# Two of eight chunks of three input projection units by seven block products, in a two-layer encoder trunk

## The chip, the cores and the metric

The kernel runs on one core of a Trainium2 chip. The metric is the device time of one execution in microseconds (us), launch to end. The core has TensorE (PE, matmuls), VectorE (DVE), ScalarE (ACT), GpSimd (POOL) and SyncE (SP, which here only issues DMAs), each with its own instruction stream; they are ordered by semaphores.

## What is computed

A trunk of two layers on 256 frames of width 2048, in float32. From the reference:

```python
for l in range(DEPTH):                       # DEPTH = 2
    h = rmsnorm(x, norm_mix[l])
    proj = h @ w_in[l]                       # 2048 -> 5456 columns
    qa, ka, va, qi, ki, wi, qb, kb, vb = jnp.split(proj, offsets, axis=-1)
    o_a = dsa_branch(...)                    # 8 heads x 128; an indexer of 16 heads x 64 keeps the 64 best keys
    o_b = swa_branch(...)                    # 16 heads x 64, window of 128, sinks
    gates = jax.nn.sigmoid(h @ w_gate[l])
    merged = g_a * (o_a @ w_branch_a[l]) + g_b * (o_b @ w_branch_b[l])
    x = x + merged @ w_out[l]
    h = rmsnorm(x, norm_mlp[l])
    x = x + jnp.square(jax.nn.relu(h @ w_up[l])) @ w_down[l]
return rmsnorm(x, final_norm)
```

The index score of a query and a key is `sum over heads of w * relu(qi . ki)`; the branch A softmax runs over the 64 keys with the best scores.

## The kernel before

**Arithmetic.** Every large product is taken in split form. A weight block arrives as `raw` in float32; ACT rounds it to `w_hi`, DVE subtracts to get `w_lo`, and TensorE adds three products of float32r: high by high, high activation by low weight, low activation by high weight. The activations are kept as such pairs too (`h_hl` for the normed input, `o_hl`, `m_hl`).

**Chunks.** All weights are cut into chunks of 256 rows by 512 columns, 1,024 columns in SBUF. A layer has 472 chunks, and every engine walks them in the same order: 8 narrow ones (`misc`: index keys, index weights, branch B keys and values), 80 of the input projection (from `C_WIN` = 8; ten units of eight), 96 of gates and branches (from `C_MIXA` = 88 and `C_MIXB` = 136), 32 of the output projection, 256 of the MLP. A unit is eight chunks that add up to 256 x 512 outputs in two PSUM banks. The units 0 and 1 of the input projection make the index queries, 2 and 3 branch A's queries, 4 and 5 its keys, 6 and 7 its values, 8 and 9 branch B's queries.

**A plain chunk** is twelve matmuls of 512 columns (L578 to L580: two row blocks of the weights, two halves of the frames, three products each). **A wide chunk** takes the 2 x 2 block product by seven block products for eight (`seven_products`, from L534): 21 matmuls of 256 columns (L546 to L548), out of sums of weight blocks (DVE, `weight_sums`, L1359 to L1365, written behind the raw block) and sums of activation blocks. It fills, beside the two banks of the unit, two side banks, which are joined with them once a unit: ACT copies half a bank, DVE makes five additions (`add_up_sides`, L1767 to L1775). Its high part is two ACT instructions (L929, L931) around the weight sums, its low part one DVE instruction of 1,792 columns (L1371); a plain chunk has one of 1,024 on each (L922, L1350). Before the change only gates of branch B and the MLP have wide chunks.

**Slots and order.** Four raw slots and four high/low slots rotate. ACT may write slot c once TensorE is through with chunk c - 4 (`multiplied`); SP issues the load of chunk c once DVE is through with chunk c - 4 (`lo_ready`); TensorE starts a chunk when its low part is there. So ACT and DVE run up to about three chunks ahead of TensorE: this is the lead that the text speaks of. Everything else is set by hand at a chunk of each engine's stream: `unit(...)` on ACT and DVE takes a `take` step (ahead of chunk 3's split), `then` steps (behind the split of the chunk given) and a `taken` step (behind chunk 6's).

**A finished unit** goes: ACT scales it out of PSUM into `stage` (`take_win`, L1128; units 6 and 7 into `va`), DVE transposes it in 32 x 32 pieces into `spread` (L1428), SP stores that in DRAM (L342) and fetches it in four parts into `moved` (L348), ACT copies it into place (`place`, L984). `stage`, `spread` and `moved` exist once. In a unit that is all done for the unit before: ACT and DVE at chunk 3, the store ahead of the load of chunk 7, the fetches behind it, ACT's `place` behind chunk 6.

**Jobs** lie between the chunks (`jobs_after`). On TensorE the index scores come in three visits of two rounds at `IDX_AT` = chunk 32, 36 and 40 of the layer (L673); ACT and DVE have their parts (relu, then a weighted sum over heads, L1507) `AHEAD` = 4 chunks further down their own streams. The top-k selection on DVE (`choose`, L1522 and L1524) stands behind chunks 52 to 60, the branch A jobs behind every other chunk from 64 on TensorE. The index scores use all four side banks (`att` 0 to 2, `turn`), branch A's jobs `att` 0 to 2, the narrow chunks `att` 0 and 1.

## Time and profile before

| | |
|---|---|
| time, median of 3 runs | 2658.05 us (2656.88 to 2658.99) |
| time of the profiled execution | 2658.03 us |
| its span, first to last instruction | 2656.1 us |
| TensorE busy | 2641.4 us (99%) |
| VectorE busy | 2078.8 us (78%) |
| ScalarE busy | 1448.1 us (55%) |
| DMA | 594.52 MB, mean 224 GB/s |
| granted TensorE clock, mean | 0.999 |

The busy time of TensorE can't be read as work at its peak: matmuls overlap in the records and their ends are modelled. What counts is the distance between the starts of two matmuls, and whether a start was held up by a semaphore. A row of the timeline says so in brackets: idle time before it and who released it. A row of several instructions (x2, x4) gives their common span.

### The profile page before, as it was taken

What the parts mean: (1) busy time and instruction counts of PE and PEld (TensorE: products, weight loads), DVE (VectorE), ACT (ScalarE), POOL (GpSimd) and SP (SyncE); (2) the same over time, 40 slices, a digit from 0 to 9 for tenths busy, and PEclk for the clock granted to TensorE, in tenths of its full rate; (3) what the DMA queues carried; (4) which work ended last, traced back from release to release, by engine and by line L of the source; (5) the groups of instructions that cost most, each with busy time, mean ns of one, the idle gap of its engine ahead of it and who ended that gap; (6) DMA issues with size and microseconds to landing.
All of it is one profiled execution on the core that took longest, in us unless ns stands there. A gap on an engine that the chain in (4) does not pass through costs nothing.

```text
span 2656.1 us, 37301 instructions
## 1 busy us (share of the span) xinstructions
PE 2641.4 (99%) x13432; PEld 2217.1 (83%) x13432; DVE 2078.8 (78%) x3099; ACT 1448.1 (55%) x1863; POOL 215.8 (8%) x378
## 2 busy tenths in 40 slices
PE   9999999999999999999999999999999999999998
PEld 7788778888888888888888887788888888888887
DVE  5667678967898897987756766789678989989875
ACT  5445555545565655655455455555456556556554
POOL 0103110000100100100010021100000001000000
PEclk9999999999999999999999999999999999999999
DMA  7877676666775766767777666667677767667574
GB/s 260 239 236 224 222 226 195 229 231 231 244 228 191 246 216 206 240 205 232 235 237 225 224 225 221 218 202 233 227 256 231 221 208 242 209 217 234 189 248 151
DMA packets 187395, 594.52 MB, mean 224 GB/s; under 512 B 25576, under 2 KB 46612, under 8 KB 187088
## 3 DMA queue, kind: packets, MB, share of 16 engines
q1 hardware_dynamic: 166256, 536.94, 62.1%
q0 software_dynamic: 20432, 54.86, 7.5%
q8 instruction: 106, 1.74, 0.3%
q14 instruction: 73, 0.60, 0.1%
q10 hardware_dynamic: 528, 0.37, 0.1%
HBM read 544.58 MB, written 47.48 MB: 223 GB/s over the span
## 4 chain that ended last, share of the span: by engine, by line
PE 95%; DVE 3%; DMA 1%; issue 1%; ACT 0%; DVEq 0%; POOLq 0%; POOL 0%; SPq 0%; ACTq 0%
PE acc L578 24%; PE acc L579 24%; PE acc L580 24%; PE att L546 2%; PE att L548 2%; PE att L547 2%; PE acc L546 2%; PE acc L548 2%; PE acc L547 2%; PE acc L595 1%; PE acc L594 1%; PE acc L596 1%; DMA raw<-in_w_main 1%; DVE w_lo L1350 1%; DVE w_lo L1371 1%
## 5 line engine op out<-in xcount | busy, mean ns | idle before, releaser
L1350 DVE TENSOR_TENSOR w_lo<-raw,w_hi 128x1024 fp32r<-128x1024 f32 (+1 forms) x778 | 933.2, 1211 | 374.0 <-ACT w_hi L922 370.3
L922 ACT ACTIVATE w_hi<-raw 128x1024 fp32r<-128x1024 f32 (+1 forms) x778 | 813.1, 1051 | 633.5 <-PE acc L580 462.4
L578 PE MATMUL acc<-w_hi,h_hl 128*128 128x512 f32 x1848 | 735.2, 398 | 1.1 <-DVE w_lo L1350 1.1
L580 PE MATMUL acc<-w_hi,h_hl 128*128 128x512 f32 x1848 | 728.9, 394 | 0.0
L579 PE MATMUL acc<-w_lo,h_hl 128*128 128x512 f32 x1848 | 728.6, 394 | 0.0
L578 PEld LDWEIGHTS acc<-w_hi,h_hl 128*128 128x128 f32 x1848 | 347.9, 188 | 83.0 <-issue 4.9
L580 PEld LDWEIGHTS acc<-w_hi,h_hl 128*128 128x128 f32 x1848 | 347.9, 188 | 81.3
L579 PEld LDWEIGHTS acc<-w_lo,h_hl 128*128 128x128 f32 x1848 | 348.2, 188 | 76.3
L1371 DVE TENSOR_TENSOR w_lo<-raw,w_hi 128x1792 fp32r<-128x1792 f32 x166 | 335.5, 2021 | 33.5 <-ACT w_hi L931 32.4
L578 PE MATMUL acc<-w_hi,o_hl 128*128 128x512 f32 x912 | 360.4, 395 | 0.0
L579 PE MATMUL acc<-w_lo,o_hl 128*128 128x512 f32 x912 | 360.0, 395 | 0.0
L580 PE MATMUL acc<-w_hi,o_hl 128*128 128x512 f32 x912 | 359.6, 394 | 0.0
L929 ACT ACTIVATE w_hi<-raw 128x768 fp32r<-128x768 f32 x166 | 140.3, 845 | 195.0 <-PE acc L548 110.1
L931 ACT ACTIVATE w_hi<-raw 128x1024 fp32r<-128x1024 f32 x166 | 174.9, 1054 | 86.9 <-DVE raw L1365 86.7
L580 PEld LDWEIGHTS acc<-w_hi,o_hl 128*128 128x128 f32 x912 | 171.8, 188 | 40.2
L578 PEld LDWEIGHTS acc<-w_hi,o_hl 128*128 128x128 f32 x912 | 171.6, 188 | 37.7 <-issue 1.4
L579 PEld LDWEIGHTS acc<-w_lo,o_hl 128*128 128x128 f32 x912 | 171.7, 188 | 36.3
L1359 DVE TENSOR_TENSOR raw<-raw 128x512 f32<-128x512 f32 x166 | 113.3, 683 | 21.2 <-issue 11.3
L455 POOL DMA_DIRECT2D scratch<-spread x30 | 16.9, 563 | 973.2 <-DVE spread L1428 973.2
L1428 DVE STREAM_TRANSPOSE spread<-stage 128x512 f32<-128x512 f32 x112 | 73.0, 689 | 21.8 <-ACT stage L1128 17.5
L1020 ACT ACTIVATE probs<-probs,low 128x128 f32<-128x128 f32 x96 | 41.0, 428 | 85.0 <-DVE sink_d L1592 43.8
L1363 DVE TENSOR_TENSOR raw<-raw 128x256 f32<-128x256 f32 x166 | 70.6, 425 | 5.8
(298 smaller groups left out, 3614.9 us busy)
## 6 DMA issues: line engine op xcount, KB each, us to landing
raw<-in_w_main SPq DMA_DIRECT2D x928, 512.0 KB, 4.3
scratch<-spread SPq DMA_DIRECT2D x37, 512.0 KB, 2.8
moved<-scratch SPq DMA_DIRECT2D x148, 128.0 KB, 3.2
scratch<-spread POOLq DMA_DIRECT2D x30, 512.0 KB, 3.5
moved<-scratch POOLq DMA_DIRECT2D x120, 128.0 KB, 5.0
scratch_p<-spread POOLq DMA_DIRECT2D x16, 384.0 KB, 4.6
moved<-scratch_p POOLq DMA_DIRECT2D x64, 96.0 KB, 4.3
raw<-in_w_misc SPq DMA_DIRECT2D x16, 336.0 KB, 4.0
```

The costliest lines, as they stand in the source:

```text
L546: nc.tensor.matmul(o, a_hi, hi[:, w], start=start, stop=False, skip_group_check=True)
L547: nc.tensor.matmul(o, a_hi, lo[:, w], start=False, stop=False, skip_group_check=True)
L548: return nc.tensor.matmul(o, a_lo, hi[:, w], start=False, stop=stop, skip_group_check=True)
L578: nc.tensor.matmul(o, a_hi, hi[:, kk], start=(k == 0), stop=False)
L579: nc.tensor.matmul(o, a_hi, lo[:, kk], start=False, stop=False)
L580: last = nc.tensor.matmul(o, a_lo, hi[:, kk], start=False, stop=fin)
L922: nc.scalar.activation(w_hi[s][:, 0:2 * width], raw[r][:, 0:2 * width], ACT.Copy).then_inc(hi_ready, 1)
L929: nc.scalar.activation(w_hi[s][:, 0:3 * HALF], raw[s][:, HALF:CW], ACT.Copy)
L931: nc.scalar.activation(w_hi[s][:, 3 * HALF:7 * HALF], raw[s][:, CW:2 * CW], ACT.Copy).then_inc(hi_ready, 1)
L1350: nc.vector.tensor_tensor(w_lo[s][:, 0:2 * width], raw[r][:, 0:2 * width], w_hi[s][:, 0:2 * width].bitcast(F32), ALU.subtract).then_inc(lo ...
L1359: nc.vector.tensor_tensor(r[:, 4 * HALF:6 * HALF].rearrange("p (k n) -> p k n", k=2), r[:, HALF:3 * HALF].rearrange("p (k n) -> p k n", k= ...
L1371: nc.vector.tensor_tensor(w_lo[s][:, 0:7 * HALF], raw[s][:, HALF:8 * HALF], w_hi[s][:, 0:7 * HALF].bitcast(F32), ALU.subtract).then_inc(lo ...
```

## The change

Chunks 1 and 5 of the units 1, 2 and 6 of the input projection become wide chunks, in both layers. What comes with it:

- `gate_sums(0)` and `gate_sums(2)`, which the gate stage makes later for itself, are also made in unit 0 (DVE behind the chunks 4 and 6, low parts behind chunk 6 and behind chunk 0 of unit 1; ACT's high parts behind the chunks 5 and 7), into a view of `o_hl`, `s_win`.
- The side banks are `att` 0 and 1 for unit 1, `att` 2 and `turn` for the units 2 and 6.
- Such a unit is taken in the unit after: ACT copies half a side bank ahead of chunk 3 (`win_side`), DVE joins behind chunk 3 (`add_win_sides`), ACT scales in place behind chunk 4 (`win_scale`), DVE transposes behind chunk 5. For the units 1 and 2 SP's store stands one unit further on, behind the load of chunk 2, the fetches behind that of chunk 3, ACT's `place` behind chunk 2.
- The index scores start at chunk 36 for 32, with ACT's and DVE's parts. They now also wait for the join of unit 2.
- The index keys, branch B's keys and two small tiles of the selection lie in `o_hl`, no longer in the upper half of raw slot 1, which the weight sums now use.
- Some waits of TensorE are added where a side bank or a sum is first used.

The diff, cut to its core:

```diff
-IDX_AT, IDX_STEP, IDX_ROUNDS = C_WIN + 24, 2, 6
+IDX_AT, IDX_STEP, IDX_ROUNDS = C_WIN + 28, 2, 6
...
+WIN_UNITS = (1, 2, 6)
+WIN_CHUNKS = (1, 5)
+A_GATES = 0
+W_SUMS = len(WIN_CHUNKS)
+EARLY_SIDES = len(WIN_UNITS) + A_GATES
+EARLY_WIDE = EARLY_SIDES * len(WIN_CHUNKS)
...
+        with nc.sbuf_tensor("o_room0", [P, 14 * SEQ], F32), nc.sbuf_tensor("kiT_kbT", [P, 2, SEQ], F32) as kiT_kbT, \
+                nc.sbuf_tensor("o_room1", [P, 8 * SEQ], F32), nc.sbuf_tensor("win_side_sum", [P, HALF], F32) as win_sum_room, \
+                nc.sbuf_tensor("o_room2", [P, 5 * SEQ], F32), nc.sbuf_tensor("ki2", [P, TT, 2, I_DIM], F32) as ki2, \
+                nc.sbuf_tensor("best8", [P, TOPK // 8, 8], F32) as best8:
+            pass
+        win_side_sum = win_sum_room[:, :]
...
+        s_win = o_hl[:, :, 10:14, :].rearrange("p a k s -> p a (k s)").rearrange("p a (b c) -> p a b c", b=W_SUMS)
...
+        win_sides = dict(zip(WIN_UNITS, (wide_acc[0], wide_acc[1], wide_acc[1])))
...
+                    then = {}
+                    if u - 2 in WIN_UNITS[0:2]:
+                        store, fetch = pass_on(l, E_QK + u - 2)
+                        then = {2: [store], 3: [fetch]}
+                    load_unit(l, C_WIN + 8 * u, 8, None if u - 1 in WIN_UNITS[0:2] else passing, then=then)
...
+            def win_sum(part, pair, i):
+                return s_win[:, part, pair // 2, i * P:(i + 1) * P]
...
+                    pe.wait_ge(up_summed, l * LAYER_SIDES + 2)
...
-                    unit(l * CHUNKS + (C_WIN + 8 * u), 8, h_lhs, acc[u % 2], win_between, win_before)
+                    hold = {1: [(1, misc_took, l + 1), (1, h_sums_took, l * LAYER_SUMS + 1), (5, h_sums_took, l * LAYER_SUMS + 2)],
+                            2: [(1, rows_out, 1)], 6: [(1, idx_relu, (l + 1) * IDX_ROUNDS)]}
+                    unit(l * CHUNKS + (C_WIN + 8 * u), 8, h_lhs, acc[u % 2], win_between, win_before, hold=hold.get(u, ()),
+                         wide=WIN_CHUNKS if u in WIN_UNITS else (), sum_of=win_sum, sides=win_sides.get(u))
...
+                def win_side(u):
+                    unit_done(l * CHUNKS + (C_WIN + 8 * (u + 1)))
+                    act.wait_ge(spread_ready, l * MOVES + (E_QK + min(u, 6)))
+                    nc.scalar.activation(stage[:, 0, HALF:NB], win_sides[u][0][:, HALF:NB], ACT.Copy).then_inc(sides_out, 1)
+
+                def win_scale(u):
+                    act.wait_ge(up_summed, l * LAYER_SIDES + WIN_UNITS.index(u) + 1)
+                    for t in range(TT):
+                        dst = stage[:, t, :] if u < 6 else va[:, t, (u - 6) * NB:(u - 5) * NB]
+                        last = nc.scalar.activation(dst, stage[:, t, :], ACT.Copy, scale=rms[:, 2 if u == 2 else 0, t:t + 1])
+                    last.then_inc(act_took, 1)
+
+                def win_sums_hi(n):
+                    act.wait_ge(h_summed, l * LAYER_SUMS + n + 1)
+                    nc.scalar.activation(s_win[:, 0, n, :], sums_f, ACT.Copy).then_inc(h_sums_hi, 1)
+
+                def early_steps(i):
+                    return lambda n: 3 * (l * LAYER_WIDE + i * len(WIN_CHUNKS) + n + 1)
...
+                    was_wide, then = u - 1 in WIN_UNITS, {}
+                    if u == 0:
+                        then = {5: lambda: win_sums_hi(0), 7: lambda: win_sums_hi(1)}
+                    if was_wide:
+                        then[4] = lambda u=u: win_scale(u - 1)
+                    if u - 2 in WIN_UNITS[0:2]:
+                        then[2] = win_place(u - 1)
                     unit(l * CHUNKS + (C_WIN + 8 * u), 8,
-                         take=(lambda u=u: take_win(u - 1)) if u else take_misc, taken=win_place(u),
-                         jobs=win_jobs(u))
+                         take=(lambda u=u: win_side(u - 1)) if was_wide else (lambda u=u: take_win(u - 1)) if u else take_misc,
+                         taken=None if u - 1 in WIN_UNITS[0:2] else win_place(u), jobs=win_jobs(u), then=then,
+                         wide=WIN_CHUNKS if u in WIN_UNITS else (),
+                         steps=early_steps(WIN_UNITS.index(u)) if u in WIN_UNITS else None)
...
+                def win_sums_lo(n):
+                    dve.wait_ge(h_sums_hi, l * LAYER_SUMS + n + 1)
+                    nc.vector.tensor_tensor(s_win[:, 1, n, :], sums_f, s_win[:, 0, n, :].bitcast(F32), ALU.subtract)\
+                        .then_inc(h_sums_took, 1)
+
+                def first_lo_second_sums():
+                    win_sums_lo(0)
+                    gate_sums(2)
...
+                def add_sides_up(g, sides, banks, i, sum_at):
+
+                    z, w = sides
+                    at = g * 2 + (l * LAYER_SIDES + i)
+                    steps = g * 6 + 3 * (l * LAYER_SIDES + i)
+                    quarters = stage[:].rearrange("p t (h c) -> p (t h) c", h=2)
+                    dve.wait_ge(sides_out, at + 1)
...
+                def add_win_sides(u):
+                    add_sides_up(0, win_sides[u], acc[u % 2], WIN_UNITS.index(u), win_side_sum)
...
+                    then = {}
+                    if u == 0:
+                        then = {4: lambda: gate_sums(0), 6: first_lo_second_sums}
+                    if u == 1:
+                        then = {0: lambda: win_sums_lo(1)}
+                    if u - 1 in WIN_UNITS:
+                        then[3] = lambda u=u: add_win_sides(u - 1)
+                        if u <= 6:
+                            then[5] = take
+                        take = None
+                    unit(l * CHUNKS + (C_WIN + 8 * u), 8, take=take, jobs=lambda c, u=u: jobs_after(l, C_WIN + 8 * u + c - AHEAD),
+                         then=then, wide=WIN_CHUNKS if u in WIN_UNITS else (),
+                         steps=early_steps(WIN_UNITS.index(u)) if u in WIN_UNITS else None)
```

The renumbered semaphore counts (`LAYER_SUMS`, `LAYER_SIDES`, `EARLY_WIDE` in the waits of the gate stage and the MLP) are left out. `gate_sums` moves up in the file unchanged, and `add_up_sides` becomes a call of `add_sides_up`.

## Rows read from the trace of the kernel before

**Rows 1.** The page: busy time of the engines, and the granted clock by slice.

```profile
PE 2641.4 (99%) x13432; PEld 2217.1 (83%) x13432; DVE 2078.8 (78%) x3099; ACT 1448.1 (55%) x1863; POOL 215.8 (8%) x378
...
PEclk9999999999999999999999999999999999999999
```

**Rows 2.** Waits of TensorE, whole span: us in total, times, longest.

```profile
PE att L578 <- DVE h_hl L1411: 1.9, 1, 1.9
...
PE acc L578 <- DVE w_lo L1350: 1.1, 1, 1.1
```

**Rows 3.** Timeline of TensorE, unit 1, chunks 17 and 23: start, us, instruction.

```profile
53.34 0.40 PE L578 MATMUL acc<-w_hi,h_hl 128*128 128x512 f32 x1
...
70.14 0.40 PE L578 MATMUL acc<-w_hi,h_hl 128*128 128x512 f32 x1
```

**Rows 4.** Timeline of TensorE, gate stage: a wide chunk and the next.

```profile
462.28 0.28 PE L546 MATMUL att<-w_hi,s_hh 128*128 128x256 f32 x1
...
464.78 0.39 PE L578 MATMUL acc<-w_hi,h_hl 128*128 128x512 f32 x1
```

**Rows 5.** The page's groups: weight loads. Before the bar the count, behind it busy, mean.

```profile
L578 PEld LDWEIGHTS acc<-w_hi,h_hl 128*128 128x128 f32 x1848 | 347.9, 188 | 83.0 <-issue 4.9
```

**Rows 6.** Timeline of VectorE in the gate stage.

```profile
440.40 0.42 DVE L1767 TENSOR_TENSOR stage<-att,stage 128x256 f32<-128x256 f32 x1
...
443.11 0.68 DVE L1359 TENSOR_TENSOR raw<-raw 128x512 f32<-128x512 f32 x1
...
446.28 2.02 DVE L1371 TENSOR_TENSOR w_lo<-raw,w_hi 128x1792 fp32r<-128x1792 f32 x1 [0.44 <-ACT w_hi L931]
448.23 0.68 DVE L1359 TENSOR_TENSOR raw<-raw 128x512 f32<-128x512 f32 x1
...
449.75 1.22 DVE L1350 TENSOR_TENSOR w_lo<-raw,w_hi 128x1024 fp32r<-128x1024 f32 x1
450.88 1.28 DVE L1718 SCALAR_TENSOR_TENSOR stage<-stage,acc 128x512 f32<-128x512 f32 x2
```

**Rows 7.** Groups of VectorE instructions: count, busy us, mean ns, idle before.

```profile
L1733 DVE TENSOR_TENSOR stage<-h_hl 128x512 f32<-128x512 f32 x8 | 5.5, 684 | 0.0
L1734 DVE TENSOR_TENSOR stage<-stage 128x128 f32<-128x128 f32 x8 | 2.3, 292 | 0.3
...
L1507 DVE SCALAR_TENSOR_TENSOR score<-stage,misc,score 128x256 f32<-128x256 f32 x30 | 14.5, 484 | 3.2 <-ACT stage L1014 2.3
```

**Rows 8.** Stretches: span, busy (count) of PE, PEld, DVE, ACT, POOL, clock, DMA share, GB/s.

```profile
40.00:120.00 80.00, 80.00 (x374) 64.14 (x374) 43.56 (x53) 38.91 (x44) 13.76 (x24) 1.00 0.86 254
```

**Rows 9.** Timeline of VectorE through the top-k selection.

```profile
150.55 1.23 DVE L1350 TENSOR_TENSOR w_lo<-raw,w_hi 128x1024 fp32r<-128x1024 f32 x1 [0.22 <-ACT w_hi L922]
...
162.12 2.36 DVE L1350 TENSOR_TENSOR w_lo<-raw,w_hi 128x1024 fp32r<-128x1024 f32 x2
...
170.64 1.30 DVE L1428 STREAM_TRANSPOSE spread<-stage 128x512 f32<-128x512 f32 x2
...
176.09 1.23 DVE L1350 TENSOR_TENSOR w_lo<-raw,w_hi 128x1024 fp32r<-128x1024 f32 x1
```

**Rows 10.** Timeline of TensorE: starts of chunks 61 and 63.

```profile
182.66 0.39 PE L578 MATMUL acc<-w_hi,h_hl 128*128 128x512 f32 x1
...
188.23 0.40 PE L578 MATMUL acc<-w_hi,h_hl 128*128 128x512 f32 x1
```

**Rows 11.** DMA issues of SyncE: store and fetches of unit 5's block.

```profile
171.97 0.33 SPq L342 DMA_DIRECT2D scratch<-spread  x1
...
174.92 1.75 SPq L348 DMA_DIRECT2D moved<-scratch  x4
```

**Rows 12.** Timeline of ScalarE: that block copied into place.

```profile
180.84 1.06 ACT L984 ACTIVATE qk<-moved 128x1024 f32<-128x1024 f32 x1 [2.43 <-DMA moved<-scratch]
```

**Rows 13.** DMA issues of SyncE, layer 1's gate stage: four fetches.

```profile
1774.56 3.05 SPq L348 DMA_DIRECT2D moved<-scratch  x4
```

**Rows 14.** Timeline of TensorE there.

```profile
1783.15 0.50 PE L578 MATMUL acc<-w_hi,h_hl 128*128 128x512 f32 x1 [1.09 <-DVE w_lo L1350]
```

More of the change, by code:

```diff
@@ L97 @@
 H_SUMS = 4
+LAYER_SUMS = W_SUMS + G_SUMS + H_SUMS
 B11, B22, B21, T1, T3, T2, T4 = range(7)
@@ L135, in trunk_kernel @@
         va = qiv[:, :].rearrange("p (t d) -> p t d", t=TT)
-        with nc.sbuf_tensor("raw1_room", [P, CW], F32), nc.sbuf_tensor("kiT_kbT", [P, 2, SEQ], F32) as kiT_kbT, \
-                nc.sbuf_tensor("ki2", [P, TT, 2, I_DIM], F32) as ki2, \
-                nc.sbuf_tensor("best8", [P, TOPK // 8, 8], F32) as best8:
-            pass
+        s_win = o_hl[:, :, 10:14, :].rearrange("p a k s -> p a (k s)").rearrange("p a (b c) -> p a b c", b=W_SUMS)
         raw1 = sb("raw1", [P, 2 * CW])
@@ L823, in gate_b @@
                          lambda: pe.wait_ge(act_took, l * ACT_UNITS + n + 14),
-                         hold=[(1, h_sums_took, l * (G_SUMS + H_SUMS) + G_SUMS)] if n == 0 else (),
+                         hold=[(1, h_sums_took, l * LAYER_SUMS + W_SUMS + G_SUMS)] if n == 0 else (),
                          wide=WIDE_GATE, sum_of=h_sum, sides=wide_acc[0])
@@ L1188, in gate_tanh @@
                 def gate_tanh(n):
[L1189 removed]
+                    act.wait_ge(up_summed, l * LAYER_SIDES + EARLY_SIDES + n + 1)
                     for t in range(TT):
@@ L1697, in take_stage, with gate_sums @@
                     spread_block(l, E_QK + u if u < 6 else E_QB + u - 8, stage)
+                def gate_sums(n):
+                    hi, lo = (h_hl[:, part, PIECES * n + 2:PIECES * n + 4, :].rearrange("p k s -> p (k s)").bitcast(F32)
+                              for part in range(2))
+                    both = stage2[:, 1, :]
+                    a11, a21, a12, a22 = (both[:, i * P:(i + 1) * P] for i in range(4))
+                    s1, s2, s3, s4 = (sums_f[:, i * P:(i + 1) * P] for i in range(4))
+                    chain.link(nc.vector.tensor_tensor(both, hi, lo, ALU.add))
+                    nc.vector.tensor_tensor(s3, a21, a11, ALU.subtract)
+                    chain.link(nc.vector.tensor_tensor(s1, a21, a22, ALU.add))
+                    chain.link(nc.vector.tensor_tensor(s2, s1, a11, ALU.subtract))
+                    nc.vector.tensor_tensor(s4, a12, s2, ALU.subtract).then_inc(h_summed, 1)
@@ new lines, in win_sums_lo, with early_steps @@
+                def win_sums_lo(n):
[5 more added lines that the diff above has]
+                    gate_sums(2)
+                def early_steps(i):
+                    return lambda n: 3 * (l * LAYER_WIDE + i * len(WIN_CHUNKS) + n)
@@ new lines, in add_sides_up @@
+                def add_sides_up(g, sides, banks, i, sum_at):
[4 more added lines that the diff above has]
+                    dve.wait_ge(sides_out, at + 1)
+                    nc.vector.tensor_tensor(sum_at, z[:, 0:HALF], quarters[:, 1, :], ALU.add).then_inc(up_step, 1)
+                    dve.wait_ge(up_step, steps + 1)
+                    nc.vector.tensor_tensor(quarters[:, 0::3, :], sum_at.unsqueeze(1).to_broadcast([P, 2, HALF]),
+                                            w[:].rearrange("p (h c) -> p h c", h=2), ALU.subtract).then_inc(up_step, 1)
+                    dve.wait_ge(up_step, steps + 2)
+                    nc.vector.tensor_tensor(quarters[:, 2, :], quarters[:, 3, :], w[:, 0:HALF], ALU.subtract).then_inc(up_step, 1)
+                    nc.vector.tensor_tensor(stage[:, 0, :], banks[0][:], stage[:, 0, :], ALU.add)
+                    dve.wait_ge(up_step, steps + 3)
+                    nc.vector.tensor_tensor(stage[:, 1, :], banks[1][:], stage[:, 1, :], ALU.add).then_inc(up_summed, 1)
@@ L1699, in _, with add_up_sides @@
+                def add_up_sides(g, n, i):
+                    add_sides_up(g, wide_acc[n // 2], acc[0], EARLY_SIDES + i, side_sum)
+                def add_win_sides(u):
+                    add_sides_up(0, win_sides[u], acc[u % 2], WIN_UNITS.index(u), win_side_sum)
                 for u in range(N_WIN):
                     take = take_keys if u == 0 else (lambda u=u: take_stage(u - 1)) if u <= 6 or u == 9 else None
-                    unit(l * CHUNKS + (C_WIN + 8 * u), 8, take=take, jobs=lambda c, u=u: jobs_after(l, C_WIN + 8 * u + c - AHEAD))
+                    then = {}
[11 more added lines that the diff above has]
+                         steps=early_steps(WIN_UNITS.index(u)) if u in WIN_UNITS else None)
@@ L1724, in take_branch_b @@
                     spread_block(l, E_M + n, stage2)
-                def gate_sums(n):
-                    hi, lo = (h_hl[:, part, PIECES * n + 2:PIECES * n + 4, :].rearrange("p k s -> p (k s)").bitcast(F32)
-                              for part in range(2))
-                    both = stage2[:, 1, :]
-                    a11, a21, a12, a22 = (both[:, i * P:(i + 1) * P] for i in range(4))
-                    s1, s2, s3, s4 = (sums_f[:, i * P:(i + 1) * P] for i in range(4))
-                    chain.link(nc.vector.tensor_tensor(both, hi, lo, ALU.add))
-                    nc.vector.tensor_tensor(s3, a21, a11, ALU.subtract)
-                    chain.link(nc.vector.tensor_tensor(s1, a21, a22, ALU.add))
-                    chain.link(nc.vector.tensor_tensor(s2, s1, a11, ALU.subtract))
-                    nc.vector.tensor_tensor(s4, a12, s2, ALU.subtract).then_inc(h_summed, 1)
                 def gate_sums_lo(n):
-                    dve.wait_ge(h_sums_hi, l * (G_SUMS + H_SUMS) + n + 1)
+                    dve.wait_ge(h_sums_hi, l * LAYER_SUMS + W_SUMS + n + 1)
                     nc.vector.tensor_tensor(s_hh[:, 1, n, :], sums_f, s_hh[:, 0, n, :].bitcast(F32), ALU.subtract)\
```

35 lines of the change are left out of this document (9 added, 26 removed).

## The prediction

> **What bounds the kernel now.** I read the page first: TensorE is busy for 99% of the span at a granted clock of nine tenths or more in every slice, VectorE (DVE) for 78% and ScalarE (ACT) for 55% [rows 1]. The waits of TensorE come next: the longest is 1.9 us, and those on a late weight block (w_lo) are 1.1 us at most [rows 2]. So the span is the length of the matmul stream, and a change is worth what it does to that stream, plus any wait that it lets in. The stream is read by the start times of matmuls, since their recorded durations overlap. In the input projection, chunk 17 starts at 53.34 us and chunk 23 at 70.14 us: six plain chunks in 16.80 us, 2.80 us each, or 233 ns for each of its twelve 512-column matmuls [rows 3]. A chunk by seven block products in the gate stage runs from 462.28 to 464.78 us: 2.50 us, or 119 ns for each of 21 matmuls of 256 columns [rows 4].
>
> **What the change removes on the path.** Units 1, 2 and 6 take chunks 1 and 5 by seven products: six chunks a layer, twelve in all. Each goes from 2.80 to 2.50 us. 12 x 0.30 = 3.6 us less of matmul stream. The score matmuls are the same ones, four chunks later, and remain on the path. The program's other matmuls are unchanged.
>
> The shorter matmuls want 21 weight loads for 12. A load is recorded with 188 ns [rows 5], which is more than the 119 ns between two matmuls, but the chunk of [rows 4] runs at that spacing with just such loads, so they are hidden and the price is already in the 2.50 us.
>
> The Trainium skill speaks against the trade: "TensorE: Matmul & The Clock Gate", section Back-to-back issue gap, gives a sustained spacing of about 81 ns at 128 columns and 131 ns at 512, so a short matmul costs more than its share. A line between the two puts 256 columns at an estimated 98 ns; 21 of these are 2.06 us against 1.57 us for twelve long ones, and the change would lose 5.9 us. The same section's spacing for a matmul alone (columns over 2.4 GHz and 2.5 ns) gives 2.29 against 2.59 us, a gain of 3.6 us. The trace agrees with the second on the difference (0.30 us a chunk), though both its spacings lie some 8% above it.
>
> **What it adds on DVE.** I take the spacing of starts in the gate stage, where each of the differences below lies between two instructions with no idle time between them [rows 6]: a plain low part 1.13 us (449.75 to 450.88), a wide one 1.95 us (446.28 to 448.23), the three weight sums 1.52 us (448.23 to 449.75), the five additions that join the side sums 2.71 us (440.40 to 443.11). So a wide chunk adds 1.52 + 0.82 = 2.34 us to DVE, and each of the three units 2.71 us for its join. The two activation sums in unit 0 are each an addition of 0.68 us and four short operations of 0.29 us [rows 7]: 0.68 + 4 x 0.29 = 1.9 us, and 0.7 us for the low part of the same width as that addition, 5.2 us for the two. ACT adds a second activation to each wide split, and swaps the two copies out of PSUM for one short copy and two scalings.
>
> Units 0 to 3 have room: in the 80 us from 40 to 120 us DVE is busy for 43.6 us and ACT for 38.9 us [rows 8]. Four wide chunks, two joins and the sums are 9.4 + 5.4 + 5.2 = 20.0 us against 36.4 us of idle time. Their cover is the lead of the weight blocks over TensorE: without it the same 20 us a layer would be on the path. I take nothing, between nothing and 1 us. Nothing can be gained there, since TensorE waits for nothing there.
>
> **Moved steps and queues.** The finished blocks of units 1 and 2 are now joined by DVE behind the low part of the next unit's chunk 3, scaled by ACT behind the split of chunk 4, and transposed by DVE behind chunk 5. Behind ACT's wait for the join stands the split of chunk 5, itself wide; behind DVE's wait for the scaling stand the low parts of chunks 6 and 7. SyncE (SP) stores such a block behind the weight load of chunk 2 of the unit after (before: ahead of that of chunk 7), so it is ready; the four fetches stand behind the load of chunk 3 and hold up the load of chunk 4. From a store to the fetches is 3.0 us [rows 11], about a chunk, so that load is hardly late. ACT's copy of the fetched block stands behind the split of chunk 2, ahead of that of chunk 3. The path from the fetches to that copy is 5.9 us (174.92 to 180.84) [rows 11, 12], two chunks. All this I cost at nothing, at most 1 us. The GpSimd queue is passed by nothing in this stage; the new waits of TensorE (side banks free, sums there, scores done, blocks joined) are for work that is ordered several chunks ahead.
>
> **Where the cover is thinnest: unit 6.** Its chunks 1 and 5 are chunks 57 and 61 of the layer, in the middle of the top-k selection. In that stretch DVE has no idle time from the low part at 162.12 to the one at 176.09 us [rows 9], so what is added there delays in full. The low part of chunk 61 starts at 176.09 and is done at 177.3, TensorE begins that chunk at 182.66 [rows 10]: a lead of 5.4 us. Ahead of its start come the sums and wide part of chunk 57 and the sums of chunk 61: 1.52 + 0.82 + 1.52 = 3.86 us, so it starts at 179.95 and ends at 181.9. TensorE is there 0.30 us sooner, at 182.36. A lead of 0.5 us is left: no wait, but barely. Chunk 63 is the second thin place: the transposes at 170.64 move by 2.34 us, with them the store (171.97), the fetches (174.92) and ACT's copy (180.84, to 183.2) [rows 9, 11, 12]; split and low part follow, 186.4 us, against TensorE at 188.23 - 0.60 = 187.6: 1.2 us left.
>
> The score rounds now end four chunks nearer to this. A round's DVE part is four operations of 484 ns and their links, 2.1 us [rows 7]. The last one falls just before the transposes of chunk 51, which wait for a copy by ACT that itself waits for the end of a unit on TensorE; I reckon it ends as that copy does, and costs nothing, at most 2.1 us.
>
> **The sum.** 2658.03 us is the profiled execution's own time, 0.02 us off the median of the runs; its span is 2656.1 us, and 1.9 us lie around it. 2658.03 - 3.6 = 2654.4 us, -0.14%.
>
> One term can go either way. In layer 1's gate stage TensorE waited 1.1 us for a weight block [rows 14], since four fetch issues of SP took 3.05 us [rows 13], against 1.75 us elsewhere [rows 11], and the DVE is full there. Such a slow issue depends on what meets it; the same work in layer 0 had none. With every queue shifted it may be gone (-1.2 us) or turn up at another of the full places (+1.2 us). I leave it in the sum.
>
> **The rivals.**
> 1. The slow issue is gone, and all else as forecast: 2653.2 us. For it: it occurred in one layer only. Against: five other places as full can meet one. 20%.
> 2. The lead at chunk 61 is overdrawn: half a microsecond more of DVE work than reckoned, or a weight load landing late (the sums now want it 1.5 us earlier), gives TensorE a wait of about 1 us a layer: 2656.4 us. For it: a lead of 0.5 us. Against: DVE durations repeat to some ten nanoseconds. 20%.
> 3. Slower than before: the last two score rounds are not hidden but push the top-k by 4.2 us. Then the lead of 0.5 us turns into a wait of 3.7 us a layer, 7.4 - 3.6 = 3.8 us more: 2661.8 us. It decides from a push of 2.3 us (1.8 us saved a layer and the 0.5 us). For it: the rounds do move onto the neighbours of the top-k. Against: ahead of chunk 52's low part, at 150.55 us, DVE still waits for ACT [rows 9], so it isn't behind there. 8%.
> 4. The wide chunk isn't shorter here, bound by its weight loads: 21 x 188 ns = 3.95 us against 2.80, 12 x 1.15 = 13.8 us more, 2671.8 us. The chunk of [rows 4] speaks against it, with the same operand shapes. 1%. This is the direction of the skill's sustained figures.
>
> **How the numbers follow.** Forecast 2654.4 us: 51%; rivals 20, 20, 8 and 1%. About 0.2% (5.3 us) is what a measurement of this kernel can tell from no change. Faster by more than that needs 1.7 us beyond the forecast: rival 1 with another 0.5 us, 10%. Slower by more takes a push of over 4.9 us a layer ((5.3 + 3.6) / 2 + 0.5), which I give half of rival 3's chance, or rival 4: 5%. Within: 85%. The range covers rivals 1 and 2 with about 1 us of spread between executions: 2652.2 to 2658.0 us.
>
> **What would show it.** Right: in the input projection wide chunks at 2.50 us, no wait of TensorE above 2 us, the low part of chunk 61 ending within 1 us ahead of its first matmul in both layers, the lead of chunks 17 to 39 above 2 us. Wrong: an idle of TensorE ahead of chunk 57, 61 or 63, a wait of the score matmuls for a join, or wide chunks over 2.6 us.

## The result, and the profile after

The changed kernel takes 2663.74 us, median of 19 runs (2658.61 to 2669.98), beside 2658.02 us (2656.51 to 2660.80) for the kernel before: 1.0022 times as long, 95% interval 1.0016 to 1.0029. I forecast 2654.4 us with a range up to 2658.0, so it came out 5.7 us slower where I had 3.6 us faster, and outside the range. The profiled execution took 2662.73 us, its span is 2660.8 us.

The page's busy times and TensorE's waits (us in total, times, longest) answer to [rows 1] and [rows 2]:

```profile
PE 2643.5 (99%) x13540; PEld 2223.3 (84%) x13540; DVE 2129.2 (80%) x3189; ACT 1458.8 (55%) x1885; POOL 215.8 (8%) x378
```

```profile
PE att L692 <- ACT stage L1036: 4.8, 3, 2.1
PE acc L544 <- DMA xs<-in_x: 1.5, 1, 1.5
PE att L784 <- DVE moved L1702: 1.3, 1, 1.3
PE att L593 <- DVE h_hl L1461: 0.6, 1, 0.6
PE att L717 <- DVE o_hl L1621: 0.5, 1, 0.5
PE att L593 <- DVE w_lo L1400: 0.3, 1, 0.3
```

The first row is new. L692 is the index score matmul, L1036 the relu by which ScalarE takes its banks. Three waits of 4.8 us together were not in the kernel before. The 1.1 us wait for w_lo at the end of [rows 2] is gone.

The wide chunks do what was forecast. Chunk 17 in TensorE's timeline of the changed kernel, which answers to [rows 3]:

```profile
55.14 0.28 PE L561 MATMUL att<-w_hi,o_hl 128*128 128x256 f32 x1
...
57.63 0.40 PE L593 MATMUL acc<-w_hi,h_hl 128*128 128x512 f32 x1
```

2.49 us from one chunk's start to the next, 2.80 before. All twelve give 0.26 to 0.31 us when the starts of equal chunks are laid beside each other. Laid so through the whole program, after against before, the profiled executions differ as follows.

| place | after minus before, us |
|---|---|
| layer 0, chunk 0, matmuls at the spacing of 1.2 GHz instead of 2.4 | +1.8 |
| 12 wide chunks | -3.6 |
| layer 0, score visit after chunk 40 | +2.3 |
| layer 0, score visit after chunk 44 | +2.3 |
| layer 0, 1.2 GHz behind that visit | +1.5 |
| layer 1, score visit after chunk 44 | +1.0 |
| layer 0, chunk 85, wait for o_hl | +0.7 |
| layer 1, gate stage, chunk 154 | -1.3 |
| small steps below 0.4 us | 0 |
| end | +4.7 |

So 7.1 us came in at three score visits, twice what the wide chunks gave.

The second of these visits, TensorE's timeline:

```profile
138.83 1.14 PE L692 MATMUL att<-kiT_kbT,qiv 64*128 64x256 f32 x8
141.91 0.48 PE L692 MATMUL att<-kiT_kbT,qiv 64*128 64x256 f32 x1 [1.95 <-ACT stage L1036]
...
142.66 0.52 PE L692 MATMUL att<-kiT_kbT,qiv 64*128 64x256 f32 x1
...
143.71 0.63 PE L594 MATMUL acc<-w_lo,h_hl 128*128 128x512 f32 x1
144.14 0.63 PE L595 MATMUL acc<-w_hi,h_hl 128*128 128x512 f32 x1
```

The first round of the visit runs, the second finds its banks not taken and waits 1.95 us. Behind it the 512-column matmuls start 427 ns apart instead of 233. The same place by stretches (span; busy of PE, PEld, DVE, ACT, POOL; granted clock; DMA share; GB/s) has the clock at 0.50, its level of 1.2 GHz:

```profile
143.00:145.00 2.00, 2.00 (x7) 1.49 (x6) 1.93 (x3) 1.72 (x3) 0.00 (x0) 0.50 0.63 112
145.00:147.00 2.00, 2.00 (x8) 1.61 (x7) 1.96 (x4) 0.11 (x1) 0.10 (x1) 0.71 0.37 126
```

Why the relu was late stands in ScalarE's timeline:

```profile
133.41 1.06 ACT L944 ACTIVATE w_hi<-raw 128x1024 fp32r<-128x1024 f32 x1 [1.73 <-PE acc L595]
139.83 1.06 ACT L1006 ACTIVATE qk<-moved 128x1024 f32<-128x1024 f32 x1 [5.35 <-DMA moved<-scratch]
140.79 0.58 ACT L1036 ACTIVATE stage<-att 128x512 f32<-128x512 f32 x1
141.27 0.59 ACT L1036 ACTIVATE stage<-turn 128x512 f32<-128x512 f32 x1
```

ScalarE sits idle for 5.35 us ahead of the copy of a fetched block (place, L1006) until the fetches land, and the two relus are the next instructions in the same queue. TensorE's second round starts 0.05 us after they end. The block is that of unit 3, which the change doesn't move. The visit before it shows the same with unit 2's block, which is moved: a copy at 124.32 us with 5.46 us idle, the relus to 126.35, TensorE at 126.41.

The kernel before has this order too, but not this wait:

```profile
108.93 1.06 ACT L984 ACTIVATE qk<-moved 128x1024 f32<-128x1024 f32 x1 [1.71 <-DMA moved<-scratch]
109.90 0.58 ACT L1014 ACTIVATE stage<-att 128x512 f32<-128x512 f32 x1
110.37 0.59 ACT L1014 ACTIVATE stage<-turn 128x512 f32<-128x512 f32 x1
```

```profile
111.58 1.34 PE L673 MATMUL att<-kiT_kbT,qiv 64*128 64x256 f32 x9
112.55 0.38 PE L673 MATMUL turn<-kiT_kbT,qiv 64*128 64x256 f32 x1
```

Its relus ended at 110.96 us, and the second round of that visit began at 112.55 us, behind the eight matmuls of the first round (the first row counts one of the second round too). The slack was 1.6 us.

### The profile page after: what moved, and what is told of

It is laid out like the page before. It is cut to its first block, busy times and chain, and to the rows that moved or that the text cites. A ratio compares the mean times of both kernels' runs of the same rounds, so it can differ in the third digit from the quotient of the medians.

```text
span 2660.8 us, 37641 instructions
## 1 busy us (share of the span) xinstructions
PE 2643.5 (99%) x13540; PEld 2223.3 (84%) x13540; DVE 2129.2 (80%) x3189; ACT 1458.8 (55%) x1885; POOL 215.8 (8%) x378
## 4 chain that ended last, share of the span: by engine, by line
PE 96%; DMA 2%; DVE 1%; issue 1%; ACT 1%; SPq 0%; POOLq 0%; POOL 0%; ACTq 0%
PE acc L593 24%; PE acc L595 24%; PE acc L594 24%; PE att L561 2%; PE att L563 2%; PE att L562 2%; PE acc L561 2%; PE acc L563 2%; PE acc L562 2%; PE acc L609 1%; PE acc L610 1%; PE acc L611 1%; DMA scratch<-spread 1%; DMA moved<-scratch 1%; PE turn L562 1%
## 5 line engine op out<-in xcount | busy, mean ns | idle before, releaser
L1400 DVE TENSOR_TENSOR w_lo<-raw,w_hi 128x1024 fp32r<-128x1024 f32 (+1 forms) x766 | 919.3, 1211 | 325.9 <-ACT w_hi L944 324.0
L944 ACT ACTIVATE w_hi<-raw 128x1024 fp32r<-128x1024 f32 (+1 forms) x766 | 798.4, 1051 | 591.8 <-PE acc L595 427.1
L593 PE MATMUL acc<-w_hi,h_hl 128*128 128x512 f32 x1800 | 717.3, 398 | 0.0
L595 PE MATMUL acc<-w_hi,h_hl 128*128 128x512 f32 x1800 | 710.8, 395 | 0.0
L594 PE MATMUL acc<-w_lo,h_hl 128*128 128x512 f32 x1800 | 710.5, 395 | 0.0
L593 PEld LDWEIGHTS acc<-w_hi,h_hl 128*128 128x128 f32 x1800 | 339.2, 188 | 79.5 <-issue 5.0
L595 PEld LDWEIGHTS acc<-w_hi,h_hl 128*128 128x128 f32 x1800 | 339.1, 188 | 79.5
L594 PEld LDWEIGHTS acc<-w_lo,h_hl 128*128 128x128 f32 x1800 | 339.6, 189 | 73.9
L1421 DVE TENSOR_TENSOR w_lo<-raw,w_hi 128x1792 fp32r<-128x1792 f32 x178 | 359.9, 2022 | 43.5 <-ACT w_hi L953 42.6
L951 ACT ACTIVATE w_hi<-raw 128x768 fp32r<-128x768 f32 x178 | 150.4, 845 | 202.8 <-PE acc L563 118.5
L953 ACT ACTIVATE w_hi<-raw 128x1024 fp32r<-128x1024 f32 x178 | 187.4, 1053 | 87.7 <-DVE raw L1415 87.5
L1409 DVE TENSOR_TENSOR raw<-raw 128x512 f32<-128x512 f32 x178 | 121.6, 683 | 12.8 <-DMA raw<-in_w_main 7.4
```

Source lines behind the costliest of these rows:

```text
L593: nc.tensor.matmul(o, a_hi, hi[:, kk], start=(k == 0), stop=False)
L594: nc.tensor.matmul(o, a_hi, lo[:, kk], start=False, stop=False)
L595: last = nc.tensor.matmul(o, a_lo, hi[:, kk], start=False, stop=fin)
L944: nc.scalar.activation(w_hi[s][:, 0:2 * width], raw[r][:, 0:2 * width], ACT.Copy).then_inc(hi_ready, 1)
L951: nc.scalar.activation(w_hi[s][:, 0:3 * HALF], raw[s][:, HALF:CW], ACT.Copy)
L953: nc.scalar.activation(w_hi[s][:, 3 * HALF:7 * HALF], raw[s][:, CW:2 * CW], ACT.Copy).then_inc(hi_ready, 1)
```

## The experiments

The theories that the experiments were to tell apart:

- A: the relus wait behind a copy that hangs on a transfer.
- B: the place of the scores, four chunks later, costs in itself.
- C: the clock of the first chunks, or other chance.
- D, a part of A: a store right behind a large load is slow.
- F, added later: the wide chunks and joins deliver the block late.

Each kernel below was timed beside the kernel before on the same chip, and a ratio is always to that one. Kernels that are compared with each other ran on one chip, unless it is said otherwise.

### Relus ahead of the copies

```diff
 # ScalarE's unit, for unit 4 alone
+                    if jobs and jobs_first:
+                        jobs(c)
                     if c in then:
                         then[c]()
...
                     if taken and c == 6:
                         taken()
...
-                    if jobs:
+                    if jobs and not jobs_first:
                         jobs(c)
```

> The changed kernel, with one order turned round: in unit 4 ScalarE makes the two relus of the index scores ahead of the copy of the moved blocks (chunks 42 and 46) instead of behind it. Theory A (the relus are queued behind a copy that waits for its transfer to land, and TensorE's next score round waits for them): the three waits of the score line for ScalarE (2.07, 1.95 and 0.75 us) and the stretch at 1.2 GHz behind the second (1.5 us) go, together 6.3 us of the 2663.7: 2657.4 us, and about 2655.6 if the first chunks, which ran at 1.2 GHz in the changed kernel's profile (1.8 us), come at 2.4 GHz as before. The three waits read below 0.1 us. Theory B (the scores are four chunks too late for VectorE and what stands behind them, or the score rounds are simply more costly there): nothing moves, 2663 us. Theory C (the loss is the cold clock of the first chunks and other disturbance that changes with each program): a time anywhere between 2655 and 2664 with the waits of the score line in place.

Measured: 2656.27 us (ratio to before 0.9994, interval 0.9985 to 1.0003). The score line doesn't appear in TensorE's waits any more, no stretch behind the visits is slow. This order alone is worth some 7 us to the changed kernel (ratios of 1.0022 and 0.9994). B is out: the scores stand where they did. C explains a part only: chunk 0 is as slow in this profile as in that of the changed kernel (1.9 and 1.8 us), and the loss is gone all the same.

In this profile the copies are as late as ever (126.27 us with 6.2 us idle), and something else shows: TensorE now reaches chunk 61 of layer 0 before its low part (a step of 0.9 us), and waits at chunks 35 and 36 of layer 1 for low parts that stand behind another late copy (0.5 and 1.1 us).

### Stores and fetches one chunk earlier

```diff
-                        then = {2: [store], 3: [fetch]}
+                        then = {1: [store], 2: [fetch]}
```

> The changed kernel, with the moved store and fetches of units 1 and 2 one chunk earlier on SyncE's queue (store behind the second load of the unit instead of the third, fetches behind the third instead of the fourth); ScalarE's order stays. Theory A (the relus hang on the landing of the fetches): the copies of units 1 and 2 are ready one chunk, 2.5 to 2.8 us, sooner; the score line's waits of 2.07 and 1.95 us in layer 0 and 0.75 us in layer 1 go and the 1.2 GHz stretch with them: 2657.4 us, or 2659.5 if the store waits for its data and gains only 1 us. Theory D, a part of it: a store that is issued 0.4 us behind a 512 KB load takes 5.3 to 6.7 us to its first fetch, against 3.4 to 4.7 us in the kernel before where it stood alone; this edit leaves a load just ahead of it, so that time stays above 5 us. Theory B (place of the scores): 2663 us.

Measured: 2655.65 us (0.9992, 0.9983 to 1.0001). Of the three waits one of 0.9 us is left. A holds from this side as well: what matters is when the transfer lands. Theory D missed its figure: the first fetch follows the store by 3.5 to 4.7 us here, not over 5. The store now stands 1.2 us behind a load and not 0.4 us, since it waits for its data.

### Both

> The changed kernel with both edits: the relus of unit 4 ahead of the copies, and store and fetches one chunk earlier. Theory A: no wait of the score line is left and the copies of units 1 and 2 come sooner for what reads them; 2655 to 2657.4 us, at or below the kernel before (2658.0), with 3.6 us from the twelve wide chunks and up to 1.8 us given to the clock of the first chunks. Theory B: 2663 us.

> The kernel with both edits once more, for its interval against the kernel before: 2655.4 us, 3 us below it, the times within 3 us of one another; no wait of the score line for ScalarE. If the low median of the first time was chance, it comes within 1 us of the kernel before.

> The kernel with both edits a third time, beside the one without wide chunks: 2.5 to 3 us below the kernel before, as the two times so far (0.9987 and 0.9993), and 3 to 4 us below the kernel that has the moves and the edits alone.

Measured: 2655.43, 2657.56 and 2657.51 us on three chips, ratios 0.9987 (0.9978 to 0.9996), 0.9993 (0.9984 to 1.0002) and 0.9985 (0.9976 to 0.9994). This version is 2.5 to 3 us faster than the kernel before; the interval of the second time alone doesn't exclude no change. It is 12 us faster than the changed kernel on the chip that ran both (2657.56 and 2669.66 us). The second time missed what was expected of it: its runs lie 6 us apart, not 3. No wait of the score line is left in any of the three profiles. In the first of them the SyncE queue (issues) and ScalarE's timeline ahead of the visit after chunk 40 read

```profile
107.77 0.33 SPq L353 DMA_DIRECT2D scratch<-spread  x1
108.88 0.33 SPq L337 DMA_DIRECT2D raw<-in_w_main  x1
112.54 1.75 SPq L359 DMA_DIRECT2D moved<-scratch  x4
```

```profile
118.72 0.58 ACT L1038 ACTIVATE stage<-att 128x512 f32<-128x512 f32 x1
119.20 0.59 ACT L1038 ACTIVATE stage<-turn 128x512 f32<-128x512 f32 x1
119.67 1.06 ACT L1008 ACTIVATE qk<-moved 128x1024 f32<-128x1024 f32 x1
120.62 1.27 ACT L1152 ACTIVATE stage<-acc,rms 128x512 f32<-128x512 f32 x2
```

with no idle time at all ahead of the copy (0.80 us in the third profile), where the changed kernel's store and fetches were

```profile
111.77 0.43 SPq L353 DMA_DIRECT2D scratch<-spread  x1
112.53 0.33 SPq L337 DMA_DIRECT2D raw<-in_w_main  x1
117.02 1.75 SPq L359 DMA_DIRECT2D moved<-scratch  x4
```

### The scores four chunks later, alone

```diff
-IDX_AT, IDX_STEP, IDX_ROUNDS = C_WIN + 24, 2, 6
+IDX_AT, IDX_STEP, IDX_ROUNDS = C_WIN + 28, 2, 6
```

> The kernel before, with the index scores, and the adds and relus with them, four chunks later and nothing else changed: no wide chunk, no moved block. Theory A (the shift matters only because the moved copy stands ahead of the relus): here the copies of units 3 and 4 stand at the end of their units as before and are on time, so no wait of the score line beyond a few tenths: 2657.5 to 2659.0 us. Theory B (the shift itself costs, by the top-k steps that wait for the last round or by VectorE's load): 2 us or more above the kernel before, 2660 to 2662 us, and the lead of the attention steps at chunks 70 to 85 falls to nothing.

Measured: 2658.45 us beside 2658.38 (1.0000, 0.9991 to 1.0009). The shift is free. TensorE is 2.1 us ahead from chunk 33 and gives it back by chunk 45; nothing else moves by more than 0.4 us. B is out a second time.

### The moves alone

```diff
 # SyncE
+                    if u - 2 in MOVED:
+                        store, fetch = pass_on(l, E_QK + u - 2)
+                        then = {2: [store], 3: [fetch]}
+                    load_unit(l, C_WIN + 8 * u, 8, None if u - 1 in MOVED else passing, then=then)
 # ScalarE
+                         taken=None if u - 1 in MOVED else win_place(u),
+                         then={2: win_place(u - 1)} if u - 2 in MOVED else {}
 # VectorE
+                    later = {5: take} if u - 1 in MOVED else {}
```

Only added lines are shown. MOVED is (1, 2); the scores are shifted too, and no chunk is wide.

> The kernel before, with no wide chunk, but with the moves of the changed kernel: the index scores four chunks later, and of the blocks of units 1 and 2 the spread on VectorE, the store and the fetches on SyncE and the copy on ScalarE where the changed kernel has them (store right behind the third load of the unit after next, copy behind the third split). Theory A (the loss lies in the queue positions alone: the relus and the splits of chunks 35 and 36 stand behind a copy that waits for its transfer): the score line waits for ScalarE again, 1 to 2.3 us at each of the visits that cost it in the changed kernel, with or without the 1.5 us at 1.2 GHz behind them: 2661 to 2665 us, against 2658.4. Theory F (the block is late because the wide chunks, side sums and joins deliver it late): without them the store has its data long before, the copy is on time, no wait above 0.3 us: 2658 to 2659.5 us.

> The changed kernel as it is, beside the others on the same chip. Theory A: 2662 to 2666 us again, with the score line waiting for ScalarE in layer 0 by some 2 us at each of two visits; since the waits hang on when a transfer lands, the times spread over 5 us or more. The first chunks at 1.2 or at 2.4 GHz (1.8 us) are as likely the one as the other: three of the six profiles so far show each.

Measured: 2663.00 us for the moves alone (1.0010, 1.0001 to 1.0019), 2669.66 us for the changed kernel (1.0034, 1.0021 to 1.0048), 2660.07 us for the kernel before. The changed kernel came out above the 2662 to 2666 us that I expected. Its profile has the score line waiting four times, 6.0 us in all, at 1.2 GHz behind both visits of layer 0. The moves alone wait once:

```profile
PE att L678 <- ACT stage L1019: 1.2, 1, 1.2
```

So neither A in its pure form nor F is right. The queue positions alone lose 2.9 us between the medians. How much of that is the wait of the scores isn't shown: the one profile, the slowest of its eleven runs, has 1.5 us at the visits, 2.0 us at the slow first chunks and the rest of its 9.7 us over the kernel before scattered over both layers. The wide chunks, which should take 3.6 us off, add 6.7 (2669.66 - 2663.00), some 10 us more than they should. Laid chunk by chunk beside the kernel before, the visits, with the slow clock behind them, cost 11.7 us in this profile of the changed kernel and 1.5 us in that of the moves alone: 10.2 us, the size of that loss. The traces give the path. ScalarE's copy of unit 1's block, ahead of the split of the chunk behind it, in the moves alone and then in the first profile of the changed kernel (the rows and times from here on are from it):

```profile
97.92 1.06 ACT L989 ACTIVATE qiv<-moved 128x1024 f32<-128x1024 f32 x1 [2.02 <-DMA moved<-scratch]
```

```profile
99.22 1.06 ACT L1006 ACTIVATE qiv<-moved 128x1024 f32<-128x1024 f32 x1 [4.83 <-DMA moved<-scratch]
```

TensorE is some 1.5 us further on in the second at that point (1.2 us of it by four wide chunks), so the same transfer is later for it, by 2.8 us of idle on ScalarE. VectorE's low parts wait for the splits behind that copy, and then it has the join to do as well, in its timeline of the changed kernel:

```profile
101.53 1.23 DVE L1400 TENSOR_TENSOR w_lo<-raw,w_hi 128x1024 fp32r<-128x1024 f32 x1 [5.89 <-ACT w_hi L944]
102.67 0.42 DVE L1781 TENSOR_TENSOR win_side_sum<-att,stage 128x256 f32<-128x256 f32 x1
...
108.97 1.30 DVE L1478 STREAM_TRANSPOSE spread<-stage 128x512 f32<-128x512 f32 x2
```

In the moves alone these transposes start at 105.47 us. The load behind which the next store stands, and with it the store, come at 111.77 instead of 108.76 us, the copy of unit 2's block at 124.32 instead of 120.36, and the relus behind it make TensorE wait. Unit 3's block, which the change doesn't move, follows: ScalarE takes it out of PSUM behind those relus, at 126.24 instead of 122.27 us, it is stored at 130.82 instead of 126.84, and its copy is the late one of the visit after chunk 44. One late transfer thus delays the next block, by way of ScalarE's and VectorE's queues. That this path is what carries the 10 us is argued from these rows; that it hangs on the places of the copy and the store is shown by the two edits.

### The moves with both edits, and no wide chunk

> The kernel before with the moves (scores four chunks later, blocks of units 1 and 2 moved) and with both edits on them (relus ahead of the copies in unit 4, stores one chunk earlier), and no wide chunk. It is what stands under the kernel with both edits, so the difference between the two is the price of the wide chunks themselves. Theory A: no wait of the score line, 2658 to 2659 us, level with the kernel before; the kernel with both edits then lies 3.6 us under it for the wide chunks, up to 1.2 us more where the stall in the gate stage of layer 1 is gone there, less the 0.6 to 0.7 us that it waits at chunks 61 and 85. If the moves cost in themselves: 2660 us or more.

Measured: 2659.30 us (0.9994, 0.9985 to 1.0003), beside 2660.39 for the kernel before and 2657.51 for the one with both edits and the wide chunks. The moves themselves are free once mended. The wide chunks are worth 1.8 us between the medians, against 3.6 forecast. The runs of either version lie 4 to 7 us apart, so 3.6 us isn't excluded. The third profile of the version with both edits has its twelve wide chunks 3.4 us shorter in sum, and new waits against them; at the top-k:

```profile
182.00 0.39 PE L561 MATMUL att<-w_hi,o_hl 128*128 128x256 f32 x1 [0.71 <-DVE w_lo L1423]
```

That is chunk 61 of layer 0, with a step of 0.9 us to the chunk before, and chunk 85 costs another 0.8. Two more waits, of 0.9 us each, stand in the MLP.

### Wide chunks in units 1 and 2 only

```diff
-WIN_UNITS = (1, 2, 6)
+WIN_UNITS = (1, 2)
```

> The kernel with both edits (relus ahead of the copies in unit 4, stores one chunk earlier), with the wide chunks of unit 6 taken back: units 1 and 2 alone, eight wide chunks in the two layers instead of twelve. If a wide chunk is worth 0.30 us and nothing else, this is 4 x 0.30 = 1.2 us slower than the kernel with both, whose median was 2655.4: 2656.6 us. TensorE waited 0.65 us at chunk 61 there (VectorE's low part of the second wide chunk of unit 6, next to the top-k work); if that wait and nothing else goes too: 2656.0 us. If unit 6's join and side sums beside the top-k cost more than they give: 2655.4 us or below.

Measured: 2659.34 us, beside 2657.56 with unit 6: 1.8 us slower, where 1.2 or 0.6 us were expected. The runs reach from 2656.2 to 2665.5 us and from 2654.6 to 2660.6, and the intervals of the two ratios overlap. So nothing speaks against unit 6 in spite of its thin cover, but that it pays for itself isn't shown.

### The slow issue in the gate stage

```diff
             first_turns(0)
-            warm(1)
+            warm(41)
```

> The kernel before with 40 more idle warm-up matmuls ahead of the first chunk: some 10 to 17 us longer for them alone, and every later instruction of TensorE 40 to 80 places further on in its stream. If the slow issue on SyncE in the gate stage of layer 1 (3.05 us for four fetches, where 1.9 us is usual, and TensorE's stall of 1.1 us behind it) comes of TensorE's own instruction fetch falling on the same moment, it goes: four fetches in 1.9 us there, and no wait of the plain matmul line for the low part of the weights in that stage. If it belongs to that place of the program whatever the stream's phase, as it did in the two kernels with an unchanged stream, it stays at 3.0 to 3.5 us with a wait of 1.1 to 1.4 us.

Measured, in a single run: 2677.97 us, of which 17.2 us are the warm-up. In the gate stage of layer 1, SyncE's queue:

```profile
1792.85 1.94 SPq L348 DMA_DIRECT2D moved<-scratch  x4
```

1.94 us, and TensorE's wait at chunk 154 is gone (a step of -1.2 us), as it is in the changed kernel. New steps of 0.8 and 1.2 us come at chunks 163 and 166 of the same layer. In the kernel before, the DMA view of 1775.0 to 1777.3 us, during the slow issue of [rows 13], lists beside the fetches

```profile
q8 instruction: 1, 0.02, 3.5%
```

This queue moves something 106 times in the run, once for each 256 of TensorE's recorded instructions (a straight line through the 106 times gives 255.9; single steps lie between 150 and 340), so I take it for TensorE's program. In the kernel before one such transfer stands at 1775.5 us, and the slow issue, 1.54 us for one fetch, begins at 1775.60. In the 13 profiles 93 of the 127 issues of SyncE above 0.7 us have one within their time or 1 us before it; of all 14,963 issues only 5% have. At the place of [rows 14] the 13 profiles part cleanly. In three, the kernel before, the scores later alone and the moves alone, such a transfer stands within the four fetches and one issue takes 1.4 to 1.9 us. In the other ten no issue takes over 0.43 us and the stall is gone. There the transfer stands elsewhere in nine, and at the very end of the last fetch in the kernel with the mended moves, whose TensorE stream has as many instructions as before. So the stall goes with how this stream falls against SyncE's issues, and not with the place; how the one slows the other isn't shown.

## Why the prediction was wrong

**What bounds the kernel** was right: TensorE's stream, and any wait let into it.

**Removed on the path** was right: 12 x 0.30 us, with every wide chunk at 2.48 to 2.52 us. Of the two rules of the Trainium skill ("TensorE: Matmul & The Clock Gate", section Back-to-back issue gap) the one for a matmul alone is borne out again on the difference, 0.30 us a chunk; by the sustained spacings these chunks would have grown by 0.49 us.

**Added on VectorE** was right in size: 2.03 us for a wide low part, and VectorE's busy time grew by 50.4 us, where the terms add up to 55. Its cover in units 0 to 3 was not. I had said that the lead of chunks 17 to 39 stays above 2 us; at chunks 35 and 36 of layer 0 it fell to 1.47 and 0.42 us, and at chunk 36 of layer 1 to 1.77.

**Moved steps and queues** is the step that failed. I costed it "at nothing, at most 1 us"; in the first profile it cost 5.6 us in the waits of three visits and 1.5 us of slow clock behind one. Three things went wrong in it.
- I took the path from store to copy from unit 5 [rows 11, 12], where a store stands alone, 3 us behind a load: 3.0 us to the fetches. The store was moved to 0.4 us behind a load of 512 KB. There the first fetch followed it by 5.3 to 6.7 us in the changed kernel's profile, against 3.4 to 4.7 us for the same two blocks in the kernel before. From the fetches to the copy were to be 5.9 us [rows 11, 12] and were 7.3 for unit 2's block (117.02 to 124.32). Store to copy was to take 8.9 us, about three chunks, and took 12.6.
- I named what stands behind SyncE's and VectorE's waits, but behind ScalarE's copy only the next split, and not the relus. ScalarE has them at every other chunk, from 36 to 46 before and from 40 to 50 after, so a pair stands at chunks 42 and 46 in both kernels. The change brought the copy of unit 2's block from 38 to 42. At 46, where unit 3's copy stands in both, the shift of the scores put relus that the visit after chunk 44 needs; before, that pair was the last, and no visit waited for it. The shift by itself was harmless (0.0 us), and so were the moved copies with the relus out of the way (2656.3 us). The moved copies without the shift weren't run.
- I wrote that TensorE's new waits are for work ordered several chunks ahead. That holds for the waits that the diff adds. The one that bit is an old one, for the relu, whose slack in the kernel before was 1.6 us; I had not measured it.

**Unit 6** was right as a sum: the low part of chunk 61 ended 0.44 us ahead of TensorE in both layers, forecast 0.5, and chunk 63 had 1.5 and 2.3 us, forecast 1.2. No wait there. In layer 1 this holds in the mended version too (0.4 us in all three profiles). In layer 0 luck had a part in it: in the mended version, where TensorE hasn't been held up at the visits, the lead is 0.05 us and chunk 61 waits in two of three profiles. That is rival 2, at 0.6 to 0.9 us and in one layer.

**The slow issue** went as in rival 1 (-1.3 us): it met something in the kernel before that it doesn't meet here.

**Rival 3** had the right sign and the wrong place. It looked for the price of the later scores in VectorE's top-k. Both chances that I gave to a time above 2658 us, 8 and 1%, belong to mechanisms that didn't occur. The missing rival was a copy on ScalarE that waits for a late transfer with the relus behind it; with the slack of 1.6 us read, it would have had a good chance.

The width was wrong with it. Here, where TensorE waits for transfers, the times spread more: 2658.6 to 2670.0 us, against 2656.5 to 2660.8 before.

## What to carry to other kernels

From this case: when a step moves, list what stands behind it in its own queue at the new place, also what another part of the same change has put there, and read the slack that each of those has now. A copy that waits for a DMA should stand behind everything that doesn't need it. Take the time of a transfer from a row where its neighbours in the queue are those of the new place; and where a faster engine runs against transfers that don't get faster, expect part of the gain to come back as waits.

## What the runs showed of the hardware

**The clock fell after waits of about 2 us, not each time.** Behind the wait of 1.95 us it stood at 0.50 from about 142.7 to 146 us. Behind the one of 2.07 us in the same profile it didn't fall, nor behind waits of 1.9 to 2.0 us ahead of chunk 0 in five profiles. In the second profile of the changed kernel it fell behind waits of 2.03 and 2.34 us, and there from the first matmul on. Waits of 0.75 and 1.2 us were followed by full speed. A fall cost another 1.5 to 3.3 us.

**The first chunk runs at either speed, by execution.** The eight transposes ahead of it in TensorE's timeline, changed kernel and then the kernel before:

```profile
5.66 1.94 PE L544 MATMUL acc<-ident,xs 128*128 128x128 f32 x8 [1.46 <-DMA xs<-in_x]
```

```profile
5.68 1.06 PE L529 MATMUL acc<-ident,xs 128*128 128x128 f32 x8 [1.48 <-DMA xs<-in_x]
```

The slow form goes on into chunk 0 in five of the twelve profiles that have the same few matmuls ahead of it (336-column matmuls 280 ns apart, not 154) and costs 1.7 to 2.3 us there. 280 to 154 is about the ratio of 427 to 233 ns, the 512-column spacings at a granted clock of 0.50 and of 1.00 above, so I take it for the level of 1.2 GHz. The clock view reads 1.00 in both forms, but only since no record of the clock stands ahead of the first one, at full speed, and the view counts the time ahead of it as full. That first record begins at 4.3 to 4.8 us in the five profiles with fast transposes, at 8.7 and 9.2 us in two with slow transposes and a fast chunk 0 (which starts at 9.1 us), and at 12.9 to 14.1 us in the five with a slow chunk 0. The version with both edits has a slow chunk 0 in one profile and not in two, so it belongs to the execution. The first line of the table above is this; that it is part of the spread of every kernel here is likely, but only profiled executions show it.

**Behind a store close to a large load the fetches came later.** The blocks of units 1 and 2, by the distance of the store from the issue of the load ahead of it: at 0.4 us it took 5.1 to 7.2 us from the store to the first fetch (sixteen cases in four profiles), at 1.2 us 3.5 to 6.3 us (24 cases), at 3 us 2.7 to 4.7 us (eight). The distance isn't all: unit 0's store in layer 1, 3 us behind a load in five profiles, took 5.3 to 6.6 us there.
